# Turning the modulation matmuls round, and re-ordering the start of a two-block transformer kernel on one Trainium2 core

## The chip, the cores and the metric

One core of a Trainium2 chip runs the whole program. The metric is the device time of one execution in microseconds (us). The core has five engines that run side by side and meet only through semaphores: TensorE (PE, with its weight loads shown as PEld), VectorE (DVE), ScalarE (ACT), GpSimd (POOL) and SyncE (SP), which here only issues transfers.

## The reference

A first block (modulated norm, gated linear attention in two directions, multiscale pooling) and a second one (two kinds of attention, a convolved feed-forward), all in float32, on x of 1024 tokens x 1024 features and a context of 256 tokens. The change touches the start of the first block:

```python
shift_x, scale_x, gate_x = split(silu(c) @ w_mod + b_mod, 3)          # w_mod: 1024 x 3072
shift_c, scale_c, gate_c = split(silu(c_ctx) @ w_mod + b_mod, 3)
hc = rmsnorm(ctx, norm_g) * (1 + scale_c) + shift_c                   # 256 x 1024
hx = rmsnorm(x, norm_g) * (1 + scale_x) + shift_x                     # 1024 x 1024
p  = h @ w_in                                                         # of hc and of hx
```

`rmsnorm(x, g)` is `x * rsqrt(mean(x*x) + eps) * g`. The keys, values and low-rank gates of the context give the first states; the pooling branch takes columns u and z of `hx @ w_in`.

## The kernel before

**Layout.** Features lie on partitions: x is `xT`, 8 tiles of 128 features x 1024 tokens; the context is `cT`, 8 tiles of 128 x 256. A product of float32 accuracy is made of three matmuls on operands split in a high part (`hi`, rounded) and a low part (`lo`, the rest): hi*hi, hi*lo, lo*hi. So `H[0]`/`H[1]` and `hc[0]`/`hc[1]` are the parts of `hx` and `hc`. A weight slab (`[128, 8, 128]`, 512 KB) is loaded raw and split by GpSimd, high part by line 393, low part by line 395, written over the raw one. There are four slots for slabs (`SLOTS`), so slab j is loaded once product j-4 is done; the fourth slot lies where the modulation weights `wm4` stand and is first loaded when quarter 4 has been used.

**Jobs.** `PRE_JOBS` lists 37 products. Jobs 0 to 2 multiply the context (24 matmuls of 256 columns). From job 3 on, products over x (u0, u1, z0, z1, ...: 48 matmuls of 512 columns) alternate with ten more context ones (`ctx` 3 to 12) and eight small pooling ones (`p`). Context jobs from 3 on are j = 4, 6, 8, 10, 12, 15, 18, 20, 22, 25. Job j writes the psum buffer `G[j % 2]`, and TensorE waits until job j-2 has been read from it: by ScalarE (`evac`), for a `p` job by VectorE (line 850, `silu_zB`), whose result ScalarE stores before it reads the next z into the same place.

**The modulation.** `w_mod` comes in six quarters of 512 output columns (2 MB each): 0 and 1 are shifts, 2 and 3 scales, 4 and 5 gates. `silp` holds silu(c) and silu(c_ctx) in columns 0 and 1 of a 128-wide stationary operand with zeros behind; a quarter is 8 matmuls (line 494) with 512 moving columns of `w_mod`, giving rows. ScalarE copies the rows out (`modulation_rows`), TensorE turns them with four transposes (line 503), VectorE copies two columns of each (`modulation_columns`). When all four of quarters 0 to 3 are there, two operations make `mod` and `gsc` (shift; gain times 1 + scale).

**The order of the work** is written by hand in one program per engine. SP: parameters, quarter 0 in four pieces, quarter 1, the context, the identity, x 0 and 1, quarter 2, x 2 and 3, quarter 3, x 4 to 7, slabs 0 to 2, quarters 4 and 5. TensorE: quarters 0 to 3, with the sum of the context's squares among them (line 512), the sums of x's squares (line 520), the spread of x's reciprocal roots over all partitions (line 524), then slab 0, quarter 4, slab 1, quarter 5, slab 2, and job 3. ScalarE: squares (line 610), and high parts with the shift added (line 658). VectorE: additions of squares (line 738), then for each of 16 tiles, context first, `normed` (line 766: tile times gain times reciprocal root) and `scaled` (line 769: the low part).

Of the kernel before, what the change touches and what calls it, by code (L numbers as in the profile page):

```python
# [153 lines left out]
def program(nc, a, out, known):  # L154
# [106 lines left out]
    def split_lo(j, slot, kt=KT):  # L261
        nc.gpsimd.wait_ge(w_hi_made, j + 1)
        nc.gpsimd.tensor_tensor(w_lo[:, slot, 0:kt, :], w_raw[:, slot, 0:kt, :],  # L263
                                w_hi[:, slot, 0:kt, :].bitcast(F32), ALU.subtract).then_inc(w_ready, 1)
# [43 lines left out]
    silp = take("silu_c", [P, KT, P])  # L308
    mrow = [take("modulation_rows0", [P, NB]), take("modulation_rows1", [P, NB])]
# [3 lines left out]
    wm5 = take("wm5", [P, KT, NB])  # L313
    fourth_at = o
    wm += [take("wm4", [P, KT, NB]), wm5]
    kept_at = o
    rbc = take("ctx_rstd", [P, TC])
    modr = take("modulation_columns", [P, 24, 2])
# [34 lines left out]
    ctx_landed, x_landed, wm_landed = sem("ctx_landed"), [sem(f"x_landed{k}") for k in range(KT)], [sem(f"wm_landed{q}") for q in range(6)]  # L353
    first_landed = [sem(f"wm0_landed{i}") for i in range(4)]
# [32 lines left out]

    def pre_split(j):

        kt = pre_src(*ALL_PRE[j])[1]  # L390
        g, hi, lo, raw = nc.gpsimd, *(t[:, 0:kt, :] for t in (*pre_w[j % SLOTS], pre_raw[j % SLOTS]))
        g.wait_ge(pre_landed[j % SLOTS], 16 * (j // SLOTS + 1))
        g.tensor_tensor(hi, raw, ones.unsqueeze(1).to_broadcast([P, kt, P]), ALU.mult).then_inc(w_hi_made, 1)
        g.wait_ge(w_hi_made, j + 1)
        g.tensor_tensor(lo, raw, hi.bitcast(F32), ALU.subtract).then_inc(w_ready, 1)
# [24 lines left out]
    NORM_TILES = [("c", k) for k in range(KT)] + [("x", k) for k in range(KT)]  # L420

    with nc.Block() as block:
        @block.sync
        def _(sp):
            def load_mod(q):
                sp.dma_start(wm[q], w_mod[q]).then_inc(wm_landed[q], 16)
# [4 lines left out]
            for i in range(4):  # L431
                sp.dma_start(wm[0][:, 2 * i:2 * i + 2, :], w_mod[0, :, 2 * i:2 * i + 2, :]).then_inc(first_landed[i], 16)
            load_mod(1)
            sp.dma_start(cT, a["ctxT"]).then_inc(ctx_landed, 16)
            sp.dma_start(ident, a["identity"]).then_inc(ident_landed, 16)
            load_x(0)
            load_x(1)
            load_mod(2)
            load_x(2)
            load_x(3)  # L440
            load_mod(3)
            for k in range(4, KT):
                load_x(k)
            for j in range(3):
                pre_load(j)
            load_mod(4)
            load_mod(5)
# [6 lines left out]
            for j in range(3, J_LR + 1):  # L454
# [3 lines left out]
                if j == 6:  # L458
                    S.wait(sp, "dve", ("scaled", "x", KT - 1))
                    sp.dma_start(inv, a["inv_count"][0]).then_inc(inv_landed, 16)  # L460
# [6 lines left out]
        def _(g):  # L467
            S.mark("pool", "silu place cleared", g.memset(silp, 0.0))
# [5 lines left out]
            S.wait(g, "dve", ("scaled", "c", KT - 1))  # L474
# [9 lines left out]
        def _(pe):  # L484
            def modulation(q):

                if q:
                    pe.wait_ge(wm_landed[q], 16)
                if q >= 2:
                    S.wait(pe, "act", ("modulation rows", q - 2))  # L490
                for k in range(KT):
                    if q == 0 and k % 2 == 0:
                        pe.wait_ge(first_landed[k // 2], 16)
                    mm = pe.matmul(U[q % 2], silp[:, k, :], wm[q][:, k, :], start=k == 0, stop=k == KT - 1)
                S.mark("pe", ("modulation", q), mm)

            def turn_modulation(q):

                S.wait(pe, "act", ("modulation rows", q))
                if q:  # L500
                    S.wait(pe, "dve", ("modulation columns", q - 1))
                for m in range(4):
                    mm = pe.transpose(G[1][:, NB + m * P:NB + (m + 1) * P], mrow[q % 2][:, m * P:(m + 1) * P], ident)
                S.mark("pe", ("modulation turned", q), mm)
            S.wait(pe, "act", "silu made")
            modulation(0)
            modulation(1)
            pe.wait_ge(ident_landed, 16)
            turn_modulation(0)
# [3 lines left out]
            modulation(2)  # L513
            turn_modulation(1)
            modulation(3)
            turn_modulation(2)
            turn_modulation(3)
# [3 lines left out]
            S.mark("pe", "x squares summed", mm)  # L521
            S.wait(pe, "dve", "x rstd diagonals")
# [3 lines left out]
            S.wait(pe, "dve", ("scaled", "c", KT - 1))  # L526
            pre_gemm(0)
            modulation(4)
            pre_gemm(1)
            turn_modulation(4)  # L530
            modulation(5)
            pre_gemm(2)
            turn_modulation(5)
            S.wait(pe, "dve", ("modulation columns", 5))
            S.wait(pe, "dve", ("scaled", "x", KT - 1))

            def ctx_gates(d):
# [4 lines left out]
                for hh in range(2):  # L542
                    S.wait(pe, "act", ("ctx gates", 0, hh) if d else ("modulation rows", 4 + hh))
# [49 lines left out]
        def _(act):  # L593
            act.wait_ge(par_landed, 16)
            S.wait(act, "pool", "silu place cleared")
            S.mark("act", "silu made", act.activation(silp[:, :, 0:2], par[:, 0:16].rearrange("p (c k) -> p k c", k=KT), ACT.Silu))

            def modulation_rows(q):
                S.wait(act, "pe", ("modulation", q))
                if q >= 2:  # L600
                    S.wait(act, "pe", ("modulation turned", q - 2))
                S.mark("act", ("modulation rows", q), act.activation(mrow[q % 2], U[q % 2], ACT.Copy))
# [8 lines left out]
            def ctx_squares():  # L611
                act.wait_ge(ctx_landed, 16)
                for i in range(2):
                    S.mark("act", ("ctx squares", i), act.activation(sq[:, i, :].rearrange("p (k t) -> p k t", k=4), cT[:, 4 * i:4 * i + 4, :], ACT.Square))
            modulation_rows(0)
            ctx_squares()
            square(0)
            square(1)
            modulation_rows(1)
# [3 lines left out]
            square(2)  # L623
            square(3)
            modulation_rows(2)
            for k in range(4, KT):
                square(k)
            modulation_rows(3)
# [26 lines left out]
            for i, (kind, k) in enumerate(NORM_TILES):  # L655
                S.wait(act, "dve", ("normed", kind, k))
                n, hi, m = (TC, hc[0], 1) if kind == "c" else (T, H[0], 0)
                S.mark("act", ("hi", kind, k), act.activation(hi[:, k, :], sq[:, i % 2, 0:n], ACT.Identity, bias=mod[:, k, m:m + 1]))
                if i == 3:
                    S.wait(act, "pe", "x squares summed")  # L660
                    S.mark("act", "x root", act.activation(rstd, G[0][:, NB:NB + TT], ACT.Sqrt, scale=1.0 / D, bias=epsc))
                if i == KT + 3:
                    modulation_rows(4)
                elif i == KT + 4:
                    evac(0)
                elif i == KT + 6:
                    evac(1)
            modulation_rows(5)
# [29 lines left out]
            for j in range(3, J_LR):  # L698
                kind, n = PRE_JOBS[j]
# [25 lines left out]
        def _(v):  # L725
# [4 lines left out]
            def modulation_columns(q):  # L730
                S.wait(v, "pe", ("modulation turned", q))
                S.mark("dve", ("modulation columns", q), v.tensor_copy(modr[:, 4 * q:4 * q + 4, :], G[1][:, NB:2 * NB].rearrange("p (m c) -> p m c", m=4)[:, :, 0:2]))

            def add_squares(k):
# [3 lines left out]
                S.mark("dve", ("squares added", k), v.tensor_tensor(acc, acc, sq[:, k % 2, :], ALU.add))  # L738
            S.wait(v, "act", ("ctx squares", 1))
            do("ctx halves", v.tensor_tensor(sq[:, 0, :], sq[:, 0, :], sq[:, 1, :], ALU.add))  # L740
            do("ctx quarters", v.tensor_tensor(sq[:, 1, 0:NB], sq[:, 0, 0:NB], sq[:, 0, NB:T], ALU.add))
            S.mark("dve", "ctx squares added", v.tensor_tensor(rbc, sq[:, 1, 0:TC], sq[:, 1, TC:NB], ALU.add))
            add_squares(1)
            modulation_columns(0)
            S.wait(v, "act", "ctx root")
            S.mark("dve", "ctx rstd", v.reciprocal(rbc, rbc))
            add_squares(2)
            add_squares(3)
            modulation_columns(1)
            for k in range(4, KT):  # L750
                add_squares(k)
            modulation_columns(2)
            modulation_columns(3)
            v.wait_ge(par_landed, 16)
            S.wait(v, "dve", ("modulation columns", 3))
# [1471 lines left out]
```

## Time and profile before

| what | us |
|---|---|
| runs | 2977.93 median of 3 (2977.16 to 2980.59) |
| the profiled execution | 2977.05, its span 2975.2 |
| TensorE starts on quarter 0 | 6.00 |
| quarter 2's matmuls start | 25.30 |
| GpSimd splits slabs 0 to 2 | 38.98 to 54.80 |
| spread of x's reciprocal roots | 60.17 |
| first `normed` of x | 63.96 |
| job 3 starts | 91.50 |

A time in the trace is counted from the start of the span. Each row of a timeline is start, duration, engine, line, operation, output <- inputs, how often, and in brackets how long the engine had been idle and what released it. In a chain a row is start, length, and the work or wait that the end hung on. PEclk is the granted clock of TensorE as a share of full speed; its two levels are 0.50 (1.2 GHz) and 1.00 (2.4 GHz). A float32 matmul leaves two records.

### The profile page before, as it was taken

How to read it: one execution, taken by the hardware profiler on the slowest of the kernel's cores; microseconds unless marked ns; L12 is line 12 of the kernel's file. 1: busy time of each engine (PE TensorE's matmuls, PEld its weight loads, DVE VectorE, ACT ScalarE, POOL GpSimd, SP SyncE). 2: the span in 40 equal slices, each digit the busy share in tenths (PEclk: the TensorE clock that was granted, in tenths of full speed). 3: DMA queues.
4: the chain of work that ended last, by engine and by line, in shares of the span. 5: the costliest groups of instructions: out<-in, count | busy, mean ns of one | idle time of the engine just before them, and what ended most of it. 6: DMA issues, size and time to landing. Idle time of an engine off the chain costs nothing.

```text
span 2975.2 us, 35037 instructions
## 1 busy us (share of the span) xinstructions
PE 2682.6 (90%) x12938; PEld 2204.3 (74%) x12938; DVE 1676.1 (56%) x1535; ACT 791.8 (27%) x990; POOL 1159.7 (39%) x461
## 2 busy tenths in 40 slices
PE   6999998998989769989879788896799999999998
PEld 3878777776777658877767677775578878888876
DVE  5765355564645543556565756558777723651653
ACT  3311143343324300123333333333123301210211
POOL 2776432323314364453202222225344434444441
PEclk8999999999999989999999999997999999999999
DMA  6222311212111233221000010101011111111111
GB/s 268 86 90 76 110 47 57 68 50 68 50 58 53 107 111 108 99 85 51 29 30 22 22 44 29 36 22 64 29 43 50 49 39 47 49 50 50 44 40 73
DMA packets 52305, 185.95 MB, mean 62 GB/s; under 512 B 6184, under 2 KB 9896, under 8 KB 51408
## 3 DMA queue, kind: packets, MB, share of 16 engines
q1 hardware_dynamic: 38064, 136.89, 13.3%
q10 hardware_dynamic: 14112, 47.23, 4.5%
q8 instruction: 95, 1.56, 0.2%
q14 instruction: 34, 0.28, 0.0%
HBM read 153.65 MB, written 26.25 MB: 60 GB/s over the span
## 4 chain that ended last, share of the span: by engine, by line
PE 71%; DVE 14%; issue 7%; ACT 4%; POOL 2%; DMA 1%; DVEq 0%; SPq 0%; ACTq 0%; POOLq 0%
PE G L232 58%; PE G L1665 3%; DVE left_over L1866 2%; PE S L972 2%; DVE tiles_in L2111 1%; DVE tiles_in L2113 1%; PE U L1651 1%; DVE A_lo L2116 1%; ACT tiles_in L2064 1%; DVE tiles_made L2109 1%; PE S L1633 1%; PE U L1010 1%; POOL H_hi L1392 1%; ACT not_taken L1758 1%; DMA wm<-w_mod 1%
## 5 line engine op out<-in xcount | busy, mean ns | idle before, releaser
L258 POOL TENSOR_TENSOR w_hi<-w_raw,ones 128x1024 fp32r<-128x1024 f32 (+1 forms) x165 | 415.2, 2517 | 1180.3 <-PE G L232 1162.3
L232 PE MATMUL G<-H_hi,w_hi 128*128 128x512 f32 x1744 | 546.4, 395 | 26.8 <-POOL H_lo L1334 23.3
L232 PE MATMUL G<-H_lo,w_hi 128*128 128x512 f32 x1744 | 538.5, 390 | 0.0
L232 PE MATMUL G<-H_hi,w_lo 128*128 128x512 f32 x1744 | 538.0, 390 | 0.0
L263 POOL TENSOR_TENSOR w_lo<-w_raw,w_hi 128x1024 fp32r<-128x1024 f32 (+1 forms) x165 | 440.9, 2672 | 12.9
L232 PEld LDWEIGHTS G<-H_hi,w_hi 128*128 128x128 f32 x1744 | 325.5, 189 | 104.7 <-POOL H_lo L1334 24.9
L232 PEld LDWEIGHTS G<-H_lo,w_hi 128*128 128x128 f32 x1744 | 328.4, 188 | 69.0
L232 PEld LDWEIGHTS G<-H_hi,w_lo 128*128 128x128 f32 x1744 | 328.0, 188 | 68.8
L232 PE MATMUL G<-A_hi,w_hi 128*128 128x512 f32 x992 | 313.4, 398 | 44.2 <-DVE tiles_made L1963 15.2
L232 PE MATMUL G<-A_lo,w_hi 128*128 128x512 f32 x992 | 309.7, 394 | 0.0
L232 PE MATMUL G<-A_hi,w_lo 128*128 128x512 f32 x992 | 309.3, 393 | 0.0
L232 PEld LDWEIGHTS G<-A_hi,w_hi 128*128 128x128 f32 x992 | 187.2, 191 | 89.9 <-DVE tiles_made L1963 18.2
L1665 PE MATMUL G<-att_v,probsT 128*128 128x128 f32 x1152 | 181.1, 304 | 72.2 <-DVE probsT L1875 52.6
L1665 PEld LDWEIGHTS G<-att_v,probsT 128*128 128x128 f32 x1152 | 153.8, 207 | 88.9 <-DVE probsT L1875 59.3
L232 PEld LDWEIGHTS G<-A_lo,w_hi 128*128 128x128 f32 x992 | 188.9, 190 | 40.2
L232 PEld LDWEIGHTS G<-A_hi,w_lo 128*128 128x128 f32 x992 | 188.8, 190 | 40.1
L2111 DVE SCALAR_TENSOR_TENSOR tiles_in<-tiles_made,par,tiles_in 128x1023 f32<-128x1023 f32 x44 | 118.2, 2686 | 82.0 <-ACT tiles_in L2064 82.0
L2064 ACT ACTIVATE tiles_in<-tiles_made,par 128x1024 f32<-128x1024 f32 x44 | 54.8, 1245 | 273.9 <-DVE tiles_made L2109 273.8
L2128 DVE TENSOR_TENSOR x<-x,G 128x1024 f32 x24 | 29.3, 1222 | 171.3 <-PE G L232 171.3
L1866 DVE TENSOR_TENSOR_SCAN left_over<-not_taken 128x128 f32<-128x128 f32 (+3 forms) x64 | 99.1, 1548 | 37.9 <-ACT not_taken L1758 37.9
L1651 PE MATMUL U<-ident,probs 128*128 128x128 f32 x576 | 92.7, 292 | 13.6 <-DVE probs L1868 12.5
L1579 POOL TENSOR_TENSOR sb_squares<-sb_squares,att_squares 128x1024 f32<-128x1024 f32 x5 | 12.8, 2560 | 213.8 <-ACT att_squares L1790 204.4
(392 smaller groups left out, 3886.6 us busy)
## 6 DMA issues: line engine op xcount, KB each, us to landing
w_raw<-w_in SPq DMA_DIRECT2D x65, 512.0 KB, 3.5
w_raw<-w_up SPq DMA_DIRECT2D x44, 512.0 KB, 3.4
pre_raw<-w_in SPq DMA_DIRECT2D x30, 512.0 KB, 3.5
wm<-w_mod SPq DMA_DIRECT2D x5, 2048.0 KB, 22.1
w_raw<-w_out SPq DMA_DIRECT2D x16, 512.0 KB, 3.8
w_raw<-w_down SPq DMA_DIRECT2D x16, 512.0 KB, 3.4
xT<-xT SPq DMA_DIRECT2D x8, 512.0 KB, 20.8
b_d<-silu_zB ACTq DMA_DIRECT2D x8, 512.0 KB, 2.6
```

Source lines behind the costliest of these rows:

```text
L232: mm = nc.tensor.matmul(dst[:, n * NB:n * NB + c], w[:, k, :], m[:, k, n * NB:n * NB + c], start=first, stop=last)
L258: eng.tensor_tensor(dst, src, ones.unsqueeze(1).to_broadcast([P, kt, P]), ALU.mult)
L263: nc.gpsimd.tensor_tensor(w_lo[:, slot, 0:kt, :], w_raw[:, slot, 0:kt, :], w_hi[:, slot, 0:kt, :].bitcast(F32), ALU.subtract).then_inc(w_r ...
L972: mm = pe.matmul(S2[:, c * CH:(c + 1) * CH], kx[:, c * CH:(c + 1) * CH], qx[:, c * CH:(c + 1) * CH], start=True, stop=True)
L1010: mm = pe.matmul(U[i % 2][:, n * DV:(n + 1) * DV], KN[d][:, c, :], V[:, c, :], start=True, stop=True)
L1392: S.mark("pool", ("b hi", k), g.tensor_tensor(H[0][:, k, :].rearrange("p (c t) -> p c t", t=P), H[1][:, k, :].bitcast(F32).rearrange("p (c ...
L1633: pe.matmul(z[:, cols], q[:, tt * P:(tt + 1) * P], Ks[hh][:, cols], start=q is Qh[hh], stop=q is Ql[hh] and tt // 4 != b)
L1651: mm = pe.transpose(U[c % 2][:, (b % 4) * P:(b % 4 + 1) * P], pr[n % 2][:, b * P:(b + 1) * P], ident)
L1665: mm = pe.matmul(G[0][:, (n % 2) * NB:(n % 2) * NB + P], pT[c % 2][:, b % 4, :], av[:, b, :], start=b == 0, stop=b == tt)
L1866: do(f"s left {n}", v.tensor_tensor_scan(left[:, T - w:T][:, ::-1], nots[:, 0:w][:, ::-1], nots[:, 0:w], 1.0, ALU.mult, ALU.bypass))
L2064: S.mark("act", f"up{g} tap {m}", act.activation(gs[:, m, :], bs[:, 0, :], ACT.Identity, bias=conv_col(0, f + (f0 + m * FT)), scale=conv_c ...
L2111: do(f"up{g} near {m}", v.scalar_tensor_tensor(y[:, 1:T], u[:, 0:T - 1], conv_col(2, k), y[:, 1:T], ALU.mult, ALU.add))
```

## The change

Four parts.

1. **The modulation's operands change places.** A quarter of `w_mod` is laid out as `[128, 4, 8, 128]` and is now the stationary operand, 32 blocks of 128 x 128; `silp` shrinks to two columns per feature tile and moves. The results come out as columns, so the copy of rows, the transposes and the copy of columns go; one operation on VectorE adds the bias for each quarter.
2. **SP's order.** Slabs 0, 1 and 2 are loaded between the quarters; the identity comes later. Quarters 1 to 3 come in two pieces, quarters 4 and 5 in one.
3. **The context is scaled ahead.** VectorE multiplies all of `cT` by the reciprocal roots at once, then applies gain and shift in two halves of four tiles; ScalarE makes each half's high part and VectorE its low part, each in one operation. These stand among the squares of x. ScalarE's context root now comes before all of x's squares, the second half's high part before the square of tile 7. On TensorE slab 0's product comes ahead of the spread.
4. **High parts on ScalarE.** For jobs 3 and 5 and all context jobs from 4 on, ScalarE makes the slab's high part, GpSimd only the low one.

```diff
-    wm = [sb(f"wm{q}", 16 * KB * q, [P, KT, NB]) for q in range(4)]
+    wm = [sb(f"wm{q}", 16 * KB * q, [P, 4, KT, P]) for q in range(4)]
...
+    HI_ON_ACT = [j for j, (kind, n) in enumerate(PRE_JOBS) if j >= 3 and (kind == "ctx" or j in (3, 5))]
+
+    def pre_hi(eng, j):
+
+        kt = pre_src(*ALL_PRE[j])[1]
+        hi, raw = pre_w[j % SLOTS][0][:, 0:kt, :], pre_raw[j % SLOTS][:, 0:kt, :]
+        eng.wait_ge(pre_landed[j % SLOTS], 16 * (j // SLOTS + 1))
+        if eng is nc.scalar:
+            S.mark("act", ("hi", "w", j), eng.activation(hi, raw, ACT.Copy))
+        else:
+            S.mark("pool", ("hi", "w", j), eng.tensor_tensor(hi, raw, ones.unsqueeze(1).to_broadcast([P, kt, P]), ALU.mult))
+
+    def pre_lo(j):
+
+        kt = pre_src(*ALL_PRE[j])[1]
+        (hi, lo), raw = (t[:, 0:kt, :] for t in pre_w[j % SLOTS]), pre_raw[j % SLOTS][:, 0:kt, :]
+        S.wait(nc.gpsimd, "act" if j in HI_ON_ACT else "pool", ("hi", "w", j))
+        nc.gpsimd.tensor_tensor(lo, raw, hi.bitcast(F32), ALU.subtract).then_inc(w_ready, 1)
...
@@ SyncE @@
+            load_mod(0, 4)
+            pre_load(0)
+            load_mod(1, 2)
+            pre_load(1)
             sp.dma_start(cT, a["ctxT"]).then_inc(ctx_landed, 16)
+            load_mod(2, 2)
+            pre_load(2)
             load_x(0)
             load_x(1)
+            load_mod(3, 2)
+            sp.dma_start(ident, a["identity"]).then_inc(ident_landed, 16)
+            for k in range(2, KT):
                 load_x(k)
+            load_mod(4, 1)
+            load_mod(5, 1)
...
@@ TensorE @@
+            def modulation(q, pieces, tiles=range(4)):
+
+                for m in tiles:
+                    if m == 0 and q >= 2:
+                        S.wait(pe, "dve", ("modulation", q - 2))
+                    if m % (4 // pieces) == 0:
+                        pe.wait_ge(wm_landed[q][m * pieces // 4], 16)
+                    for k in range(KT):
+                        mm = pe.matmul(U[q % 2][:, 2 * m:2 * m + 2], wm[q][:, m, k, :], silp[:, k, :], start=k == 0, stop=k == KT - 1)
+                if 3 in tiles:
+                    S.mark("pe", ("modulation", q), mm)
             S.wait(pe, "act", "silu made")
+            modulation(0, 4)
+            modulation(1, 2)
+            modulation(2, 2, (0, 1))
             S.wait(pe, "pool", "ones made")
             S.wait(pe, "dve", "ctx squares added")
             S.mark("pe", "ctx squares summed", pe.matmul(G[0][:, 0:TC], ones, rbc, start=True, stop=True))
+            modulation(2, 2, (2, 3))
+            modulation(3, 2)
...
+            S.wait(pe, "dve", ("ctx low", 1))
+            pre_gemm(0)
             S.wait(pe, "dve", "x rstd diagonals")
...
+            modulation(4, 1)
             pre_gemm(1)
+            modulation(5, 1)
             pre_gemm(2)
...
@@ ScalarE @@
+            def ctx_high(h):
+                S.wait(act, "dve", ("ctx normed", h))
+                ks = slice(h * HALF, (h + 1) * HALF)
+                S.mark("act", ("ctx high", h), act.activation(hc[0][:, ks, :], cT[:, ks, :], ACT.Copy))
...
             S.mark("act", "ctx root", act.activation(rbc, G[0][:, 0:TC], ACT.Sqrt, scale=1.0 / D, bias=epsc))
+            square(0)
+            square(1)
+            ctx_high(0)
+            for k in range(2, KT - 1):
                 square(k)
+            ctx_high(1)
+            square(KT - 1)
...
+            for k in range(KT):
+                S.wait(act, "dve", ("normed", k))
+                S.mark("act", ("hi", k), act.activation(H[0][:, k, :], sq[:, k % 2, :], ACT.Identity, bias=mod[:, k, 0:1]))
+                if k == 2:
                     evac(0)
+                elif k == 3:
+                    pre_hi(act, 4)
+                elif k == 5:
+                    pre_hi(act, 3)
                     evac(1)
+            pre_hi(act, 5)
             evac(2)
...
             for j in range(3, J_LR):
+                if j + 3 in HI_ON_ACT:
+                    pre_hi(act, j + 3)
...
@@ VectorE @@
+            def ctx_normed(h):
+                for k in range(h * HALF, (h + 1) * HALF):
+                    i = v.tensor_scalar(cT[:, k, :], cT[:, k, :], gsc[:, k, 1:2], mod[:, k, 1:2], ALU.mult, ALU.add)
+                S.mark("dve", ("ctx normed", h), i)
```

## Rows read from the trace of the kernel before

**Rows 1.** Page, part 2: busy tenths of TensorE in 40 equal slices.

```profile
PE   6999998998989769989879788896799999999998
```

**Rows 2.** Stage windows: length, busy us of PE, PEld, DVE, ACT, POOL; PEclk; DMA; GB/s.

```profile
44.00:60.00 16.00, 1.45 (x13) 1.36 (x13) 15.68 (x15) 3.20 (x7) 10.64 (x5) 0.58 0.40 168
...
92.00:196.00 104.00, 103.14 (x527) 88.22 (x526) 80.28 (x36) 24.61 (x33) 85.99 (x32) 1.00 0.25 83
196.00:208.00 12.00, 7.73 (x37) 6.60 (x38) 11.83 (x7) 2.58 (x3) 11.84 (x5) 0.86 0.44 170
```

**Rows 3.** The chain that ended last, in order of time, up to job 3.

```profile
6.73 18.53 DMA wm<-w_mod
...
47.48 5.11 DVE sq L766 x2
...
60.17 3.76 PE S L524 x4
...
65.69 4.32 PE G L232 x24
...
85.96 5.42 DVE H_lo L769 x2
...
91.50 11.20 PE G L232 x48
```

**Rows 4.** Timeline of TensorE: modulation quarters, and both streams of one-column matmuls.

```profile
6.00 8.66 PE L494 MATMUL U<-wm,silu_c 128*128 128x512 f32 x16 [6.00 <-DMA wm<-w_mod]
...
43.60 1.84 PE L520 MATMUL G<-ones,squares_added 128*128 128x1 f32 x16
...
80.37 7.03 PE L494 MATMUL U<-wm,silu_c 128*128 128x512 f32 x16
...
2951.82 3.57 PE L2048 MATMUL G<-ones,tiles_made 128*128 128x1 f32 x16 [1.10 <-DVE tiles_made L2136]
```

**Rows 5.** Short windows around those streams and the spread; PEclk is third from last.

```profile
46.00:48.00 2.00, 0.00 (x0) 0.00 (x0) 1.96 (x2) 0.00 (x0) 1.92 (x2) 0.67 1.00 418
...
62.00:64.00 2.00, 1.92 (x3) 0.34 (x1) 0.04 (x1) 0.00 (x0) 0.00 (x0) 0.56 0.00 0
64.00:66.00 2.00, 0.32 (x2) 0.32 (x3) 1.97 (x3) 0.73 (x1) 0.31 (x2) 1.00 0.02 4
...
2954.00:2955.00 1.00, 1.00 (x6) 1.00 (x7) 0.00 (x0) 0.00 (x0) 0.00 (x0) 0.50 0.00 0
...
2956.00:2957.00 1.00, 0.30 (x2) 0.30 (x3) 0.71 (x1) 0.65 (x1) 0.00 (x0) 0.50 0.00 0
```

**Rows 6.** Timeline: who starts when a transfer lands, and SP's issue of slab 3.

```profile
17.72 2.00 ACT L614 ACTIVATE sq<-cT 128x1024 f32<-128x1024 f32 x2 [2.43 <-DMA cT<-ctxT]
...
77.26 13.37 SPq L386 DMA_DIRECT2D pre_raw<-w_in  x4
...
81.19 2.37 POOL L393 TENSOR_TENSOR w_fourth_hi<-pre_raw,ones 128x1024 fp32r<-128x1024 f32 x1 [14.29 <-DMA pre_raw<-w_in]
```

**Rows 7.** Timeline: durations of operations on ScalarE and VectorE.

```profile
26.56 1.06 ACT L610 ACTIVATE sq<-xT 128x1024 f32<-128x1024 f32 x1 [0.97 <-DMA xT<-xT]
...
60.94 0.48 DVE L766 SCALAR_TENSOR_TENSOR sq<-cT,gsc,ctx_rstd 128x256 f32<-128x256 f32 x1
...
63.96 1.28 DVE L766 SCALAR_TENSOR_TENSOR sq<-xT,gsc,S 128x1024 f32<-128x1024 f32 x1 [2.13 <-PE S L524]
...
2941.41 0.74 DVE L2133 TENSOR_SCALAR x<-x,par  x1
```

**Rows 8.** Timeline: two additions on VectorE, and TensorE's waits near 200 us.

```profile
121.71 1.23 DVE L829 TENSOR_TENSOR pool_work<-pool_sums 128x1024 f32<-128x1024 f32 x1
122.97 3.32 DVE L831 TENSOR_TENSOR pool_work<-pool_work,inv_count 128x1024 f32<-128x1024 f32 x1
...
198.36 0.35 PE L232 MATMUL G<-hc_hi,w_third_hi 128*128 128x256 f32 x1 [3.22 <-DVE silu_zB L850]
...
203.36 0.89 PE L232 MATMUL G<-H_hi,w_fourth_hi 128*128 128x512 f32 x2 [1.90 <-ACT silu_zB L653]
```

More of the change, by code:

```diff
@@ L473, in _ @@
                 pre_split(j)
-            S.wait(g, "dve", ("scaled", "c", KT - 1))
+            S.wait(g, "dve", ("ctx low", 1))
             S.mark("pool", "ctx low rank cleared", g.memset(lrc, 0.0))
@@ L542, in ctx_gates @@
                 for hh in range(2):
-                    S.wait(pe, "act", ("ctx gates", 0, hh) if d else ("modulation rows", 4 + hh))
+                    S.wait(pe, *(("act", ("ctx gates", 0, hh)) if d else ("dve", ("modulation", 4 + hh))))
                     for h in range(2):
@@ L594, in _ @@
             act.wait_ge(par_landed, 16)
[L595 to L602, printed above, removed]
+            S.mark("act", "silu made", act.activation(silp, par[:, 0:16].rearrange("p (c k) -> p k c", k=KT), ACT.Silu))
             def square(k):
@@ L622, in _ @@
             S.mark("act", "ctx root", act.activation(rbc, G[0][:, 0:TC], ACT.Sqrt, scale=1.0 / D, bias=epsc))
[L623 to L626, printed above, removed]
+            square(0)
+            square(1)
+            ctx_high(0)
+            for k in range(2, KT - 1):
                 square(k)
-            modulation_rows(3)
+            ctx_high(1)
+            square(KT - 1)
+            S.wait(act, "pe", "x squares summed")
+            S.mark("act", "x root", act.activation(rstd, G[0][:, NB:NB + TT], ACT.Sqrt, scale=1.0 / D, bias=epsc))
             def evac(j):
@@ L728, in do, with modulation @@
                 S.wait(v, "dve", name)
-            def modulation_columns(q):
-                S.wait(v, "pe", ("modulation turned", q))
-                S.mark("dve", ("modulation columns", q), v.tensor_copy(modr[:, 4 * q:4 * q + 4, :], G[1][:, NB:2 * NB].rearrange("p (m c) -> p m c", m=4)[:, :, 0:2]))
+            def modulation(q):
+                S.wait(v, "pe", ("modulation", q))
+                ms = slice(4 * q, 4 * q + 4)
+                bias = par[:, R0["bm"] + 4 * q:R0["bm"] + 4 * q + 4]
+                S.mark("dve", ("modulation", q), v.tensor_tensor(mod[:, ms, :], U[q % 2][:, 0:8].rearrange("p (m c) -> p m c", c=2), broadcast(bias.unsqueeze(2), 2), ALU.add))
+                if q in (2, 3):
+                    S.wait(v, "dve", ("modulation", q))
+                    gain = par[:, R0["ng"] + 4 * (q - 2):R0["ng"] + 4 * (q - 2) + 4]
+                    do(("norm scales", q), v.scalar_tensor_tensor(gsc[:, 4 * (q - 2):4 * (q - 2) + 4, :], mod[:, ms, :], 1.0, broadcast(gain.unsqueeze(2), 2), ALU.add, ALU.mult))
             def add_squares(k):
@@ L742, in _ @@
             S.mark("dve", "ctx squares added", v.tensor_tensor(rbc, sq[:, 1, 0:TC], sq[:, 1, TC:NB], ALU.add))
+            modulation(1)
+            S.wait(v, "act", "ctx root")
+            do("ctx rstd", v.reciprocal(rbc, rbc))
+            do("ctx scaled", v.tensor_tensor(cT, cT, rbc.unsqueeze(1).to_broadcast([P, KT, TC]), ALU.mult))
             add_squares(1)
-            modulation_columns(0)
-            S.wait(v, "act", "ctx root")
-            S.mark("dve", "ctx rstd", v.reciprocal(rbc, rbc))
+            modulation(2)
@@ L747, in _ @@
+            ctx_normed(0)
             add_squares(2)
-            add_squares(3)
-            modulation_columns(1)
-            for k in range(4, KT):
+            ctx_low(0)
+            for k in range(3, KT - 1):
                 add_squares(k)
[L752 to L755, printed above, removed]
-            do("shift, scale", v.tensor_tensor(mod[:, 0:16, :], modr[:, 0:16, :], broadcast(par[:, R0["bm"]:R0["bm"] + 16].unsqueeze(2), 2), ALU.add))
@@ L757, in _ @@
-            do("norm scales", v.scalar_tensor_tensor(gsc, mod[:, 8:16, :], 1.0, broadcast(par[:, R0["ng"]:R0["ng"] + KT].unsqueeze(2), 2), ALU.add, ALU.mult))
-            def norm_step(i, second):
-                kind, k = NORM_TILES[i]
-                n, src, hi, lo, m, r = (TC, cT, *hc, 1, rbc) if kind == "c" else (T, xT, *H, 0, S2)
-                t = sq[:, i % 2, 0:n]
+            modulation(3)
+            ctx_normed(1)
+            add_squares(KT - 1)
+            ctx_low(1)
+            S.wait(v, "act", "x root")
@@ L762, in norm_step @@
+            v.wait_ge(ident_landed, 16)
+            do("x rstd", v.reciprocal(rstd, rstd))
+            S.mark("dve", "x rstd diagonals", v.tensor_tensor(diag, ident.unsqueeze(1).to_broadcast([P, TT, P]), broadcast(rstd.unsqueeze(2), P), ALU.mult))
+            def norm_step(k, second):
+                t = sq[:, k % 2, :]
                 if not second:
-                    if kind == "x" and k == 0:
-                        S.wait(v, "pe", "x rstd spread")
-                    S.wait(v, "dve", ("scaled", *NORM_TILES[i - 2]) if i >= 2 else ("squares added", KT - 1))
@@ L770, in _ @@
+            S.wait(v, "pe", "x rstd spread")
             norm_step(0, False)
-            for i in range(len(NORM_TILES)):
-                if i == 5:
-                    S.wait(v, "act", "x root")
-                    do("x rstd", v.reciprocal(rstd, rstd))
-                    S.mark("dve", "x rstd diagonals", v.tensor_tensor(diag, ident.unsqueeze(1).to_broadcast([P, TT, P]), broadcast(rstd.unsqueeze(2), P), ALU.mult))
-                if i + 1 < len(NORM_TILES):
-                    norm_step(i + 1, False)
-                if i == KT + 5:
-                    modulation_columns(4)
-                norm_step(i, True)
@@ L781, in _ @@
-            modulation_columns(5)
-            S.wait(v, "dve", ("modulation columns", 5))
-            S.mark("dve", "gate", v.tensor_tensor(mod[:, 16:24, :], modr[:, 16:24, :],
-                                                  broadcast(par[:, R0["bm"] + 16:R0["bm"] + 24].unsqueeze(2), 2), ALU.add))
+            for k in range(KT):
+                if k + 1 < KT:
+                    norm_step(k + 1, False)
+                if k == 5:
+                    modulation(4)
+                norm_step(k, True)
```

123 lines of the change are left out of this document (32 added, 91 removed).

## Prediction

> **What bounds the kernel now.** I read the page first, for where the span goes: TensorE is busy nine tenths of it, and the first slices are the poor ones [rows 1]. Everything the diff touches lies before about 340 us, so next came the stage windows [rows 2]. They show two weak places: 44 to 60 us, where TensorE does 1.45 us of work, and 196 to 208 us, where it does 7.7 of 12. Between and behind them TensorE is full (103.1 of 104 us from 92 to 196). So only two things count: when the first large product, job 3, can start (91.50 us now), and what holds TensorE up near 200 us. The chain that ended last says what leads to 91.50 [rows 3]: transfers of w_mod, TensorE on the modulation, VectorE on squares and the context's norm, the spread of x's reciprocal roots, then TensorE and VectorE in turn, the last link being H_lo.
>
> **The modulation's products.** Before, a quarter q is 8 matmuls with 512 moving columns, each two records of 0.43 us at the full clock: 7.0 us at 80.37 [rows 4]. Only the first quarter starts slowly (8.66 us). Its turning (four transposes, a copy on ScalarE, one on VectorE) goes, 6 times; all but the last lay under other quarters, so I count nothing for it. In their place stand 4 x 8 = 32 matmuls a quarter, each with a full 128x128 fp32 weight load and two moving columns. The trace has this shape twice, with one moving column: 8 matmuls in 1.84 us at 43.60 (0.23 us each) and 8 in 3.57 us at 2951.82 (0.446 us each) [rows 4]. The weight load sets both, so two columns cost what one does. A quarter is then 32 x 0.23 = 7.4 us at the high level of the clock and 32 x 0.446 = 14.3 us at the low one. The high one would be no loss. The low one costs 7.3 us a quarter, and these are the two ends of the bound.
>
> Which level applies decides the case. Dense streams raised the clock: the spread began at 60.17 after nearly 15 idle us, and the windows from 62 and from 64 us read 0.56 and 1.00 [rows 5]. After the thin stream at 43.60, which TensorE entered at 1.00 and straight out of transposes, it fell: 0.67 over 46 to 48. The thin stream at 2951.82 kept TensorE occupied without a gap for 3.6 us, and the window at its end and the one after still read 0.50 [rows 5]. Neither place is as long as a quarter, so this is strong but not proof. The new kernel starts cold (the first matmuls of the quarter at 6.00 ran at half speed) and begins with thin matmuls. I take the low level for quarters 0 to 3.
>
> The Trainium skill's page "TensorE: Matmul & The Clock Gate", Part 1, says the opposite for a TensorE kept busy: activity releases the throttle, without distinguishing wide from thin matmuls. By that rule the 32 matmuls would run at 0.23 us and the time would be that of the first rival below; the rows at 2951.82 speak against it here.
>
> **Transfers.** SP's order puts two slabs of 0.5 MB ahead of the context and one more ahead of x. The context landed at 17.72 with 5.1 MB before it, quarter 2 at 25.3 with 8.2 MB [rows 3, 6]: 2.5 us a MB. So in the new order the context lands at 20.2, quarter 3 at 34, the last tile of x (14.7 MB) at 41. TensorE at the low level needs quarter 3 only at 49, so none of this is on the path; at the high level it is, by up to 3.6 us for x. Splitting slabs 0 to 2 on GpSimd then falls at 12 to 31 us and costs nothing. Before, it stood at 39 to 55 beside VectorE's small operations, which it made slow (two 256-column ones took 5.11 us, later ones 0.48 each) [rows 3, 7]. That gain comes before the wait for quarter 3, and so is lost with it.
>
> **Sum to job 3, low level.** TensorE starts at 6.0; four quarters 57.2; the context's sum in their midst 0.9 (two records of 256 columns at half speed): 64.1. ScalarE's context root is queued ahead of all squares of x, and it waits for that sum (42.6); squares 0 to 6 and their additions still finish by about 61, under quarter 3. From 64.1 the new order is a plain chain: modulation and scales 0.5; four scalings of 256 columns 1.2 (bounds: a quarter of the 0.74 us of a 1024-column TENSOR_SCALAR, and the 0.48 of the old 256-column operation); context high part 1.06; square of tile 7 1.06, queued behind it; its addition 1.24 [rows 7]: 69.2. The x sums are thin matmuls, 3.6: 72.8. Slab 0's product now stands ahead of the spread on TensorE: 24 matmuls, 4.3 as it was to 5.1 all at half speed [rows 3]; I take 5.0: 77.8. The spread: 3.76 before, half that at the high level; 2.5: 80.3. So x's norm starts at 80.3 and not at 63.96, 16.3 us late.
>
> Behind that TensorE has quarter 4, slab 1, quarter 5, slab 2. Quarters 4 and 5 cost between 14.8 and 28.6 together. The dense products ahead of each lift the clock for part of it, as the spread did; I take 22, slabs 1 and 2 take 9 (5.8 to 10.2): 111.3.
>
> VectorE meanwhile makes eight tiles of x at 2.56 us each (1.28 twice) [rows 7]. ScalarE now stops at tile 3 for slab 4's high part. Queued behind that wait are the high parts of tiles 4 to 7, for which VectorE's low parts wait. Slab 4's load is issued behind slab 3's, and SP holds that until quarter 4 is done (91.3); before, the issue at 77.26 landed for GpSimd at 81.19, 3.9 us [rows 6]. With the second slab 1.3 us later, slab 4 is there at 96.5, its high part at 97.6, tile 4's at 98.7, and the last low part at 98.7 + 1.3 + 3 x 2.56 + 1.4 (slab 3's high part and an evacuation on ScalarE) = 109, plus up to 4 for GpSimd's low parts beside it. The two engines end together; job 3 starts at 111.3, against 91.50: +19.8.
>
> **What comes back after it.** Ten context slabs and jobs 3 and 5 leave GpSimd's high part (2.37 us at best) to ScalarE (1.06) [rows 6, 7]. ScalarE is busy 25 of 104 us there [rows 2], and where its new wait for a landing precedes an evacuation, a product of 10.9 us or a short pool product covers it. VectorE gains: an addition of two 1024-column tiles takes 1.23 us, but 3.32 beside GpSimd [rows 8]. At 198.36 TensorE had waited 3.22 us for VectorE's silu_zB, at 203.36 another 1.90 for ScalarE's, which waits for its store, and the clock fell (0.86 over the stretch, 1.7 us lost) [rows 2, 8]: 6.8 us in all. To remove it VectorE must be 5.4 us earlier. Of GpSimd's ten operations in its way, jobs 17 to 21, two go (18 and 20), which is two collisions of 2.1 us; the first wait ends with that, and with it probably the fall of the clock. Bounds 0 and 6.8; I take 5.
>
> So +19.8 - 5.0 = +14.8. The profiled execution took 2977.05 (span 2975.2 and 1.85 around it), 0.9 below the median of the runs: 2991.9, or 2992.7 by the median; I say 2992. That is half a per cent; 0.2% (6 us) is about what the measurement can tell.
>
> **Rivals.**
> *The clock rises although the matmuls are thin* (0.14; ends faster). Then TensorE follows the transfers: quarter 3 done at 39, x's squares at 50.6 behind the context's high part, norm from 61.5, slab 4's high part at 75.2, last tile at 85.4 to 90. Job 3 starts 1.5 to 6.1 us early, with 5 from the second place: about -9, 2968. It decides if two quarters out of the first four run at 0.23. For it: nothing idles; against it: both thin places [rows 4, 5].
> *Low for quarters 0 to 3, high for 4 and 5* (0.13). The dense work at 73 to 80 would carry it. TensorE then needs 20.6 and not 31 us, but VectorE's wait for slab 4 (load at 87.7, last tile near 107) binds: +15.5 - 5, 2987 to 2988.
> *ScalarE's wait for slab 4 ends last and the stall near 200 us stays* (0.14). Every low part of tiles 4 to 7 beside GpSimd, as the 5.42 us for two before 91.5 [rows 3], gives 115: +23.5, 3000.
> *The likeliest*, as summed: 0.55. Something else 0.04.
>
> **Numbers.** The likeliest case's own ends: quarters 4 and 5 nearly all at the low level and nothing regained, +27, 3004; VectorE binding at 107 and 7 regained, +8.5, 2985. I go to 2983 to 3004, which leaves out mainly the first rival. Faster by over 0.2%: the first rival less its slow edge, 0.13; within: its edge and the other cases', 0.10; slower 0.77.
>
> **What would show it.** In the changed profile: the modulation's records near 0.22 us apart and the granted clock 0.50 from 6 to 64 us; quarter 3's end near 64; x's norm starting near 80; ScalarE idle at tile 4, put down to a slab's transfer; job 3 near 111; TensorE's waits for silu_zB gone or under 2 us. The prediction is wrong if the clock reads 1.00 in the first 40 us (then TensorE waits for w_mod), or if two columns cost other than one.

## The result, and the profile after

The changed kernel takes 2996.3 us (median of 4, 2993.24 to 3001.24) against 2977.55 for the kernel before: ratio 1.0066, 95% interval 1.0046 to 1.0085, slower by 14 to 25 us. The profiled execution took 3001.24, its span 2999.4. Ratios compare fast runs only, which leaves out one execution of cols128 (an experiment below) that took 7450 us.

The chain that ended last, in the kernel after, from the first matmul to the first products over x (the last row is slab 2 and job 3 together):

```profile
5.31 34.26 PE U L506 x160
39.58 1.06 PE G L515 x2
40.64 20.29 PE U L506 x96
...
61.68 1.06 DVE cT L739 x3
...
63.73 1.05 ACT sq L600
...
64.80 1.24 DVE squares_added L735
...
66.08 3.58 PE G L520 x16
69.66 4.27 PE G L232 x24
73.93 1.72 PE S L526 x4
75.64 10.03 PE U L506 x64
85.67 4.72 PE G L232 x24
90.39 11.02 PE U L506 x64
101.41 16.24 PE G L232 x72
```

It answers to [rows 3, 4]. One engine and one line, L506, carry the start: 160 records in 34.26 us are 0.214 us each, and a quarter (64 records) is 13.7 us, where it was 7.0. After the first matmul no transfer of w_mod is on the chain any more: the weights wait for TensorE. The norm of x starts at 75.68 (63.96 before), job 3 at 106.54 (91.50 before).

Windows of the same kernel, the first from quarters 2 and 3, the others around quarters 4 and 5 (columns as in [rows 2], PEclk third from last):

```profile
40.00:50.00 10.00, 10.00 (x48) 9.91 (x46) 6.98 (x9) 3.25 (x4) 0.00 (x0) 1.00 1.00 426
...
76.00:78.00 2.00, 2.00 (x20) 2.00 (x20) 2.00 (x2) 1.00 (x1) 0.00 (x0) 1.00 0.00 0
...
82.00:84.00 2.00, 2.00 (x11) 2.00 (x11) 1.99 (x2) 0.90 (x2) 0.00 (x0) 0.50 0.00 0
...
90.00:92.00 2.00, 2.00 (x21) 2.00 (x19) 0.00 (x0) 1.40 (x2) 0.00 (x0) 1.00 0.25 61
...
96.00:98.00 2.00, 2.00 (x11) 2.00 (x10) 2.00 (x1) 0.51 (x1) 2.00 (x2) 0.50 0.00 0
```

Quarter 4 begins at 1.00, just behind the dense spread: 20 records in 2 us. It falls to 0.50 while TensorE and its weight loads are busy for all of the window, and then 2 us hold 11 records. Slab 1 raises the clock, quarter 5 lets it fall again. Up to 72 us the column reads 1.00 although the records are as far apart as at 0.50 (48 in the 10 us from 40): the trace has no clock event before the first change, which comes at 72.4 us within slab 0, so for that stretch the pace of the records has to be read, not the column. From 72.4 to 79.3 us the level is the high one in both.

Near 210 us, SP, ScalarE and TensorE of the kernel after ([rows 8] for before). First the timeline, then TensorE's waits from 100 to 360 us (total, times, longest):

```profile
209.69 0.33 SPq L384 DMA_DIRECT2D pre_raw<-w_in  x1
210.06 0.43 SPq L478 DMA_DIRECT2D inv_count<-inv_count  x1
...
211.26 0.33 ACTq L693 DMA_DIRECT2D b_d<-silu_zB  x1
...
216.18 1.28 ACT L645 ACT_TABLE_LOAD   x1 [3.48 <-DMA b_d<-silu_zB]
```

```profile
PE G L232 <- ACT silu_zB L645: 4.2, 1, 4.2
PE G L232 <- DVE silu_zB L855: 1.3, 1, 1.3
```

The wait for VectorE fell from 3.22 to 1.3 us, and the one for ScalarE rose from 1.90 to 4.2. The clock fell again behind the second wait, as it had before:

```profile
220.00:222.00 2.00, 2.00 (x6) 1.63 (x5) 0.00 (x0) 0.03 (x1) 2.00 (x2) 0.50 0.01 4
```

### The profile page after: what moved, and what is told of

Same layout as the page of the kernel before. It is cut to its first block, busy times and chain, and to the rows that moved or that the text cites. A ratio compares the mean times of both kernels' runs of the same rounds, so it can differ in the third digit from the quotient of the medians.

```text
span 2999.4 us, 35538 instructions
## 1 busy us (share of the span) xinstructions
PE 2715.3 (91%) x13202; PEld 2265.4 (76%) x13202; DVE 1650.1 (55%) x1529; ACT 798.2 (27%) x990; POOL 1117.3 (37%) x448
## 4 chain that ended last, share of the span: by engine, by line
PE 72%; DVE 13%; issue 7%; ACT 4%; POOL 2%; DMA 1%; DVEq 0%; ACTq 0%; SPq 0%; POOLq 0%
PE G L232 58%; PE G L1670 3%; PE U L506 3%; DVE left_over L1871 2%; PE S L977 2%; DVE tiles_in L2116 1%; DVE tiles_in L2118 1%; PE U L1656 1%; DVE A_lo L2121 1%; ACT tiles_in L2069 1%; DVE tiles_made L2114 1%; PE U L1015 1%; PE S L1638 1%; POOL H_hi L1397 1%; ACT not_taken L1763 1%
## 5 line engine op out<-in xcount | busy, mean ns | idle before, releaser
L232 PE MATMUL G<-A_hi,w_hi 128*128 128x512 f32 x992 | 314.4, 399 | 43.1 <-DVE tiles_made L1968 15.2
```

The costliest lines, as they stand in the source:

```text
L232: mm = nc.tensor.matmul(dst[:, n * NB:n * NB + c], w[:, k, :], m[:, k, n * NB:n * NB + c], start=first, stop=last)
```

## The experiments

Twelve kernels. All edits lie in the first 350 us. There the traces repeat closely: three kernels that differ only behind job 3 (changed, inv_late, store_slots) start it at 106.54, 106.27 and 106.11. The time of the whole scatters more: by 9 to 19 us between the executions of one kernel, where there were eight or more. So each is read first by two marks: when job 3 starts, and when GpSimd splits the first slab of the next stage. Each mark comes from one profiled execution, and differences of half a microsecond between marks say nothing.

| kernel | job 3 | next stage | between | time, ratio to before (95%) |
|---|---|---|---|---|
| before | 91.50 | 339.11 | 247.6 | 2977.55 |
| changed | 106.54 | 354.34 | 247.8 | 1.0066 (1.0046 to 1.0085) |
| part1_alone | 109.20 | 356.67 | 247.5 | 1.0049 (1.0031 to 1.0067) |
| hi_on_pool | 106.63 | 352.90 | 246.3 | 1.0038 (1.0024 to 1.0053) |
| cols32 | 106.65 | 355.48 | 248.8 | 2991.39, one run |
| cols64 | 101.24 | 352.04 | 250.8 | 2995.09, one run |
| cols128 | 86.51 | 336.59 | 250.1 | 0.9993 (0.9982 to 1.0004) |
| late_slab4 | 84.56 | 335.20 | 250.6 | 2974.94, one run |
| spread_first | 108.85 | 357.21 | 248.4 | 2999.76, one run |
| inv_late | 106.27 | 350.92 | 244.7 | 2986.14, one run |
| store_slots | 106.11 | 348.75 | 242.6 | 2992.37, one run |
| before_store_slots | 91.57 | 335.43 | 243.9 | 1.0009 (0.9994 to 1.0024) |
| best | 84.00 | 326.63 | 242.6 | 0.9966 (0.9954 to 0.9978) |
| best_hi_pool | 84.21 | 328.10 | 243.9 | 0.9990 (0.9977 to 1.0004) |

### Is it the clock, or the weight loads?

**cols128**: the same 32 weight loads a quarter, with 128 columns moved.

```diff
-    silp = take("silu_c", [P, KT, 2])
+    silp = take("silu_c", [P, KT, P])                       # cleared, two columns filled
...
-  mm = pe.matmul(U[q % 2][:, 2 * m:2 * m + 2], wm[q][:, m, k, :], silp[:, k, :], ...)
+  mm = pe.matmul(U[q % 2][:, P * m:P * m + P], wm[q][:, m, k, :], silp[:, k, :], ...)
```

> The changed kernel, with silu_c kept 128 columns wide (two real ones, 126 zeros), all moved: same 32 weight loads a quarter, 128 moving columns in place of 2. Theory (the low clock under thin matmuls is the whole loss): the records come about 0.11 us apart and not 0.214 once the clock is up, a quarter takes 7.1 us and not 13.7, quarter 3 ends near 40, waiting for its transfer, job 3 starts at 86 to 90 in place of 106.5; time 2974 to 2981. Rival A (the weight load sets 0.214 us whatever the clock): quarters stay at 13.7 us, 2996. Rival B (wider moving costs more than it saves): a quarter over 13.7 us, above 3000.

TensorE's timeline in that kernel:

```profile
5.30 16.48 PE L507 MATMUL U<-silu_c,wm 128*128 128x128 f32 x128 [5.30 <-DMA wm<-w_mod]
...
31.84 7.38 PE L507 MATMUL U<-silu_c,wm 128*128 128x128 f32 x64 [0.74 <-DMA wm<-w_mod]
...
62.05 7.31 PE L507 MATMUL U<-silu_c,wm 128*128 128x128 f32 x64
...
86.51 1.22 PE L232 MATMUL G<-H_hi,w_fourth_hi 128*128 128x512 f32 x2 [4.26 <-DVE H_lo L781]
```

Sixty-four times the moving columns, and a quarter takes 7.3 us and not 13.7: rivals A and B are out, and 0.214 us is not a price of the weight load alone. Now TensorE waits for w_mod, as before the change, and job 3 starts 20.0 us earlier than in the changed kernel. The time is the kernel before's within its interval (0.9993): the one number 2 for 128 is the whole loss. At the second mark the gain is 17.8 us and not 20.0, because job 3 itself now takes 13.40 us, against 11.11 in the changed kernel: behind the 4.26 us wait it starts at the low level (0.50 over 86 to 88 us).

**cols32** and **cols64** move 32 and 64.

> As the run with 128 moving columns, with 32 moved. The weight loads are the same. If the clock follows how much streams through the array, 32 columns lie between: theory says still at the low level, records 0.214 us apart, job 3 near 106; the rival (any wider operand will do) says 0.11 us and job 3 below 92.

> As the runs with 32 and 128 moving columns (32: records 0.214 us apart, job 3 at 106.7; 128: 0.119 us once up, job 3 at 86.5), with 64 moved. Theory (what streams through the array decides, not the weight loads): between the two; a clock that does not rise in the first 60 us gives job 3 near 106, one that does gives 86.5. I expect the low level. Rival: the rise at 128 columns came from something that 64 have too, and job 3 is at 86 to 88.

Timelines of quarter 4 with 32 columns, and of the start and quarter 4 with 64:

```profile
75.83 10.02 PE L507 MATMUL U<-silu_c,wm 128*128 128x32 f32 x64
```

```profile
6.02 34.37 PE L507 MATMUL U<-silu_c,wm 128*128 128x64 f32 x160 [6.02 <-DMA wm<-w_mod]
...
76.66 7.25 PE L507 MATMUL U<-silu_c,wm 128*128 128x64 f32 x64
```

With 32 job 3 and all before it are as with 2 (106.65). With 64 the start is as slow (0.215 us a record for 34 us), yet after the dense slab 0 and spread quarter 4 keeps the high level to its end. In this kernel a stream that did not raise the clock did hold it. I had expected quarter 4 to be slow too; job 3 came 5 us earlier than forecast, and then it was held by H_lo (a 4.4 us wait).

### Which part of the diff?

**part1_alone**: the kernel before with only the operands changed round (32 matmuls of two columns; ScalarE's copy of rows and the transposes gone, VectorE's copy of columns kept).

> The kernel before with part 1 alone: quarters as 32 matmuls of two columns, order of all engines as before. Theory: four quarters of 13.7 us end near 60, the context's norm begins there and not at 47.5, the spread comes near 71, and with quarters 4 and 5 at 10 to 13.7 us each job 3 starts at 105 to 112 in place of 91.5: 2992 to 2998. Rival (parts 2 and 3, the new order with its wait of ScalarE and slab 0 ahead of the spread, cause the loss): 2976 to 2981.

Job 3 at 109.20: part 1 alone makes the kernel slower, by more at the second mark (+17.6 us) than the whole change (+15.2). Parts 2 to 4 give 2.4 us back there; the time of the whole does not resolve that (1.0049 and 1.0066, with overlapping intervals).

**spread_first**: slab 0's product behind the spread again.

```diff
-            S.wait(pe, "dve", ("ctx low", 1))
-            pre_gemm(0)
             S.wait(pe, "dve", "x rstd diagonals")
             ... # the spread
+            S.wait(pe, "dve", ("ctx low", 1))
+            pre_gemm(0)
```

> The changed kernel with the spread ahead of slab 0's product again. Theory (TensorE, without a gap from the x sums on, sets job 3 in the changed kernel): x's norm starts 2 to 3 us earlier than 75.7, and job 3 stays within 1.5 us of 106.5, since TensorE has the same work and a gap of 2 us more before the spread. Rival: the norm sets job 3, and it comes 2 to 3 us earlier.

A miss in both numbers: the norm of x started 0.6 us earlier and not 2 to 3 (75.05), and job 3 2.3 us later. Slab 0's product had raised the clock for the spread (1.72 us there); with thin sums and a wait in front of it the spread took 3.41.

**late_slab4**: in cols128, slab 4's high part behind ScalarE's last tile.

```diff
-                elif k == 3:
-                    pre_hi(act, 4)
...
+            pre_hi(act, 4)
             pre_hi(act, 5)
```

> The kernel with 128 moving columns, and slab 4's high part made after ScalarE's last tile of x, not behind tile 3. In the 128-column kernel job 3 started at 86.5, after a 4.3 us wait for VectorE's last low part, and ScalarE had waited for the slab from 69.8 to 74.3. Theory: with TensorE no longer late this wait sets job 3, and without it job 3 starts at 82 to 84.5 (then TensorE's slab 2, done at 82.2, holds it). Rival: VectorE is late for another reason, GpSimd's low parts beside it, and job 3 stays within 1 us of 86.5.

The chain of cols128 shows what was taken away: the transfer of the slab between two tiles of the norm.

```profile
69.78 4.45 DMA pre_raw<-w_in
...
74.25 1.06 ACT w_hi L394
75.31 1.05 ACT H_hi L651
...
76.39 1.29 DVE H_lo L781
```

Job 3 came 2.0 us earlier, at the edge of what was expected, and still waited 2.16 us for H_lo. So the wait for the slab is real but shows only when TensorE is on time. In the changed kernel it was 6.1 us long (until 90.60) and hidden.

### Why did nothing come back near 200 us?

**hi_on_pool**: part 4 undone, `HI_ON_ACT = []`.

> The changed kernel without part 4: all high parts of slabs on GpSimd, none on ScalarE. Theory: TensorE sets job 3 (it ran without a gap from slab 0's product on), so ScalarE's 6.1 us wait for slab 4 costs nothing and the removal gives nothing there: job 3 within 1 us of 106.5. Near 212 us TensorE waits 5 to 8 us in either kernel; VectorE was 2.0 us earlier with part 4 but the store took 2.3 longer. Time within 3 us of the changed kernel, 2996. Rival A (the wait for slab 4 is what ends last): job 3 by 104, 2993 or less. Rival B (part 4 gives what I forecast): 4 to 5 us more, 3001.

Its chain beside the same pieces of the changed kernel's:

```profile
208.42 3.31 DVE kc L862
...
212.36 1.28 DVE silu_zB L851
213.66 2.58 DMA b_d<-silu_zB
```

```profile
208.08 1.24 DVE kc L866
...
209.95 1.28 DVE silu_zB L855
211.26 4.86 DMA b_d<-silu_zB
```

Part 4 does what it should for VectorE: one operation beside GpSimd less, 2.1 us. The store then takes 2.3 us longer. Both rivals are out: job 3 stays at 106.63, and without part 4 nothing is lost behind it. There TensorE waits 3.2 and 0.6 us and not 1.3 and 4.2, and the stretch between the marks is 1.5 us shorter (246.3 against 247.8): in the changed kernel part 4 costs a little.

**inv_late**: SP loads the next inv_count only when z job n-2 has been read.

> The changed kernel; SP also waits for ScalarE's reading of z job n-2 before it loads the next inv_count. Near 212 us the changed kernel's store b_d took 4.86 us beside that load (issued 1.2 us before it), and 2.58 with all high parts on GpSimd, where they lay 3.1 us apart. Theory (the 2.0 us that VectorE gained was lost to two transfers of 0.5 MB meeting): the store takes 2.6 to 2.9 us, TensorE's second wait there falls from 4.2 to about 2, and the products behind it start 2.2 us earlier relative to job 3. Rival (the store is slow for another reason, ScalarE's own copy of a slab's high part behind it): store still 4.9, nothing moves. Job 3 as before, 106.5.

The store took 3.42 us and TensorE's wait was 2.7, not the 2.6 to 2.9 and 2 expected: slab 20's load, issued at 209.37, still lay beside it. But 3.1 us are gained between the two marks, more than the two waits shrank by (1.7); the clock now stays at 1.00 there (190 to 228 us), which it did not in the changed kernel. In the changed kernel the store had met two transfers of its own size, the slab's (209.69) and inv_count's (210.06): VectorE's earliness had moved it onto them. In the run without part 4 the same two were issued 3.5 and 3.1 us ahead of it.

**store_slots** and **before_store_slots**: a semaphore for each place, so z job 2 waits for one store and not for both.

```diff
...
-                        act.wait_ge(b_stored, 32 * (n // 2))
+                        act.wait_ge(b_stored[n % 2], 16 * (n // 2))
...
```

> The changed kernel with a semaphore for each of the two places of silu_zB, so that z job 2 waits for the store of pool job 0 and not for that of pool job 1. Theory: ScalarE then waits only for VectorE's pool job 1; its table load and silu follow the issue of the store and slab 20's high part, TensorE's wait before job 19 falls from 4.2 us to 1 or less, and the clock does not fall. 3.5 to 5 us less in all from job 3 to the end of this stage. Rival: the time is only moved to the next wait (job 19 on its slab's low part), less than 1 us.

> The kernel before with a semaphore for each place of silu_zB and nothing else. Theory: of its two waits near 200 us the first, 3.22 us for VectorE, stays; the second, 1.90 us for ScalarE's silu, goes, and the clock does not fall (1.7 us): 3 to 4 us less, next stage's first slab at 335 to 336 in place of 339.1, ratio 0.9985 to 0.999. Rival: the clock falls all the same, 1.9 us or less.

In the changed kernel the waits shrink to 1.2 and 0.7 us, the clock does not fall, and the stretch between the marks shrinks by 5.2 us. In the kernel before it shrinks by 3.7, as expected, yet the time of the whole does not follow (1.0009; 0.9985 to 0.999 expected). That miss is taken up below.

### Together

> Four edits together: 128 moving columns; slab 4's high part late; a semaphore for each place of silu_zB; and the spread of the reciprocal roots ahead of slab 0's product on TensorE, as in the kernel before. The last is worth 3 to 4 us to the norm of x (diagonals ready at 56.8 in the 128-column kernel, spread at 60.3). Theory: job 3 at 79 to 83, then 3.5 to 5 us less near 200 us: 12 to 16 us below the kernel before, ratio 0.994 to 0.996. Rival: TensorE's own work (slabs 0 to 2 and quarters 4 and 5, 29 us behind the spread) holds job 3 at 86 or more, ratio 0.997 to 1.000.

> The best kernel without part 4: all slabs' high parts on GpSimd. There job 3 started at 84.0 and TensorE waited 1.1 and 0.7 us near 190 us. Theory (part 4 does give VectorE 2 us there, as between 209.95 and 212.36 in the two thin kernels, and here nothing takes it back): job 3 within 1 us of 84.0, then 2 us or a little more lost near 190: first slab of the next stage split at 328 to 330 and not 326.6; time 1 to 4 us over best. Rival: with both stores apart part 4 is worth nothing, 326.6 and the same time.

Best starts job 3 at 84.00, 1 us behind the expected span, and TensorE waits 1.1 and 0.7 us near 190: 12.5 us less at the second mark, and 0.9966 for the whole, a little under the expected gain. Its chain shows the next limit: no wait from the spread on.

```profile
57.66 3.59 PE S L525 x4
61.25 2.88 PE G L232 x24
64.12 7.15 PE U L507 x64
71.27 2.87 PE G L232 x24
74.14 7.15 PE U L507 x64
81.29 13.78 PE G L232 x72
```

Ahead of the first mark only the spread's place sets best apart from late_slab4. The norm of x starts 1.1 us earlier for it (61.29 and 62.40), not the 3 to 4 us expected, and job 3 starts 0.6 us earlier (84.00 and 84.56). It does more behind the mark. In late_slab4 and cols128 TensorE waits 2.16 and 4.26 us for H_lo and then makes job 3 in part at the low level; in best nothing is waited for, and job 3 takes 11.07 us. The chains of late_slab4 and of cols128, and one window of late_slab4 and of best:

```profile
84.56 12.76 PE G L232 x48
```

```profile
86.51 13.40 PE G L232 x48
```

```profile
84.00:86.00 2.00, 1.44 (x3) 1.16 (x4) 2.00 (x3) 1.43 (x4) 1.79 (x1) 0.63 0.80 246
```

```profile
84.00:86.00 2.00, 2.00 (x11) 1.67 (x10) 1.80 (x3) 0.45 (x2) 2.00 (x2) 1.00 0.33 100
```

So of the 8.0 us by which the stretch between the marks is shorter in best than in late_slab4, 1.7 are job 3. The rest is near 190 us: 3.7 from the two waits (4.4 and 1.1 before), and an estimated 2.7 from the clock, which reads 0.50 in late_slab4 for 5.5 busy us behind 198.42 and stays at 1.00 in best. Without part 4 the first wait near 190 is 3.2 us again and the second mark 1.5 later, as expected; the time of the whole is further off than that (0.9990 against 0.9966).

## Why the prediction was right, term by term

| term | forecast | measured |
|---|---|---|
| TensorE's start | 6.0 | 5.31 |
| quarters 0 to 3 | 57.2 | 54.6 |
| context's sum in their midst | 0.9 | 1.06 |
| from quarter 3 to the x sums | 5.1 | 5.1 |
| x sums | 3.6 | 3.58 |
| slab 0 | 5.0 | 4.27 |
| spread | 2.5 | 1.72 |
| quarters 4 and 5 | 22 | 21.05 |
| slabs 1 and 2 | 9 | 9.85 |
| job 3, against before | +19.8 | +15.0 |
| given back after it | -5.0 | +0.2 |
| sum | +14.8 | +15.2 |

**The level of the clock** was the step that decided, and it held: the low one from the start through quarter 3, part of both for quarters 4 and 5. It was read from the pace of the records, since the column says nothing there. One of the two thin places that spoke for it was weak: in the window from 46 to 48 us of [rows 5] TensorE stood idle, so the stream at 43.60 need not have been what made the clock fall; the place at 2951.82 carried the argument. The first rival (0.14) is what cols128 shows, job 3 at 86.5; its own condition, thin matmuls that raise the clock, did not come true. The Trainium skill's page "TensorE: Matmul & The Clock Gate", Part 1, lets activity release the throttle; in these runs a TensorE without gaps was not enough (34 us at the low level with 2 columns).

**The price of a thin matmul** was taken from 8 matmuls that include their start and end (0.446 us); in a long stream it is 0.428. That is 2.6 of the 4.8 us by which job 3 came earlier than forecast.

**That ScalarE's wait for slab 4 ends with TensorE** was half right. The landing came at 90.6, not 96.5, and the last low part near 102.7, not 109, so it lay hidden.

**"I take 5"** is the step that failed. The reason given, two collisions less for VectorE, was right for one of them (2.0 us of the 4.2). What the step left out is what a faster VectorE starts earlier: its store fell onto the loads of a slab and of inv_count. The profile before held the clue, a store of 2.6 us with inv_count's issue 3 us ahead of it. And the fall of the clock, 1.7 us of the 5, did not go: it follows the second wait, which grew. So the second half of the third rival came true, the stall near 200 us stayed, and the sign "TensorE's waits for silu_zB gone or under 2 us" failed.

So the sum of 14.8 is close to 15.2 by luck: two errors of 5 us have opposite signs. Without the one or the other the forecast would have been +10.0 or +20.0, both still within the stated range.

**A sign of mine was wrong**: I wrote that a clock of 1.00 in the first 40 us would refute the forecast. The column does read 1.00 there, without meaning it.

**Left open.** The medians differ by 18.8 us and the marks by 15.2, which lies within the interval of 14 to 25 us; whether the rest is real is not shown. before_store_slots and best_hi_pool gained 3.7 and 11.0 us at the second mark, and here the time disagrees: their intervals allow a gain of at most 2 and 7 us. Behind 350 us nothing is changed in any kernel, but the distance between two traces moves there in steps: at 301, 521, 1396 and 1849 us of the kernel before, ScalarE of the changed kernel is 15.3, 13.5, 18.9 and 23.1 us behind.

The record says what such differences go with. The 48 executions of the unchanged kernel that ran beside the experiments took 2968.1 to 2985.5 us at mean granted clocks from 0.964 down to 0.957, and the two are correlated (-0.76). Over the 14 traces the stretch behind the second mark lasts 2633.4 to 2645.1 us, and TensorE is at the low level for 187 to 229 us of it (correlation 0.88, about 0.3 us longer for each further microsecond at the low level). So the same work took longer where more of it fell on the low level. What makes that time differ between two executions, and whether an earlier or later start of the stage has a part in it, no run here shows.

## What to carry to other kernels

Before matmuls are turned so that a thin operand moves, price them at both levels of TensorE's clock, from a stream of the same shape in the trace, and look at the granted clock behind it: a busy TensorE did not keep it up here, and moving 126 useless columns of zeros was 20 us cheaper at job 3. Look behind a wait too: after waits of 2.2 and 4.3 us the next product took 1.7 and 2.3 us longer here, as it began at the low level. When an engine is made faster, write down what it issues next and what else is on the queues at that new time. Where a wait counts two transfers together and needs only one, a second semaphore gave 5.2 and 3.7 us at the next stage's mark, though for the kernel before that did not show in the time.

## What the runs showed of the hardware

- Float32 matmuls with a full weight load and from 2 to 128 moving columns took the same time at the same level of the clock: 0.214 us a record at the low one (2, 32 and 64 columns, streams from 5 to 40 us), 0.11 at the high one (64 and 128 columns, 7.1 to 7.4 us for 64 records; 2 columns, 20 records from 76 to 78 us).
- From the start of the program, gapless streams with 2, 32 and 64 moving columns ran 34 us at the low level; with 128 the level rose (18 records from 9 to 11 us, 11 from 7 to 9). Behind dense products the streams with 2 and 32 fell back (quarter 4 in 10.0 us), those with 64 and 128 did not (7.3). No rule for other widths or mixtures follows.
- A store of 0.5 MB took 2.58 us where the loads of a slab and of inv_count, 0.5 MB each, had been issued 3.5 and 3.1 us before it (hi_on_pool). It took 3.42 us where only a slab's load had been, 1.4 us before it (inv_late), and 4.86, 5.16 and 5.76 us where both had been, the slab's about 1.5 and inv_count's about 1.1 us before it (changed, cols128, cols32).
